# Two chained transformer blocks in float32r halves on one core: TensorE's operands placed at multiples of 64 bytes, the first weight panel on SyncE's queue, weight splits taken out of two waits of the mix stage

## The reference

```python
y = rmsnorm(h, norm_g[layer, 0])
y = gmlp_mixer(y, ...)        # layer 0
y = diff_attention(y, ...)    # layer 1
h = h + rmsnorm(y, norm_g[layer, 1])
y = conv_ffn(rmsnorm(h, norm_g[layer, 2]), ...)
h = h + rmsnorm(y, norm_g[layer, 3])
...
x = x + 0.5 * swiglu(rms_norm(x, ffn1_norm), ...)
u = rms_norm(x, mix_norm) @ w_in
x = x + concatenate([mla_attention(...), moba_attention(...)]) @ w_out
x = x + 0.5 * swiglu(rms_norm(x, ffn2_norm), ...)
return rms_norm(x, final_norm)
```

## Time and profile before

| | before |
|---|---|
| median of 3 runs | 1079.1 us (1078.93 to 1079.15) |
| the profiled execution | 1078.4 us, its span 1076.5 us |
| TensorE matmuls | busy 1064.8 us (99%), 5976 of them |
| TensorE weight loads | busy 910.5 us (85%) |
| VectorE | busy 773.5 us (72%) |
| ScalarE | busy 653.1 us (61%) |
| GpSimd | busy 35.5 us (3%) |
| DMA | 198.13 MB, mean 184 GB/s |
| granted TensorE clock | 0.997 on average |

### The profile page before, as it was taken

How to read it: one execution, slowest core, us unless ns; L and a number is a source line. 1 busy time by engine, 2 the same in 40 slices (tenths; PEclk the granted TensorE clock), 3 DMA queues, 4 the chain that set the end, 5 groups by cost and what they waited for, 6 DMA issues and landing times.

```text
span 1076.5 us, 15631 instructions
## 1 busy us (share of the span) xinstructions
PE 1064.8 (99%) x5976; PEld 910.5 (85%) x5976; DVE 773.5 (72%) x1213; ACT 653.1 (61%) x1176; POOL 35.5 (3%) x39
## 2 busy tenths in 40 slices
PE   8999999999999999999999999999999999999997
PEld 7988888888799878888888888888899878888886
DVE  5888977878767889777788655665676857565554
ACT  5767766557757777566667545545566647454453
POOL 0830000000000000000000000000000000000000
PEclk9999999999999999999999999999999999999999
DMA  9763866566463347555554755556355516565651
GB/s 349 257 209 128 249 201 199 187 189 202 164 223 112 111 161 243 187 200 187 182 190 146 234 198 186 176 192 219 122 174 156 196 59 206 186 183 192 194 174 40
DMA packets 56777, 198.13 MB, mean 184 GB/s; under 512 B 6576, under 2 KB 8536, under 8 KB 56704
## 3 DMA queue, kind: packets, MB, share of 16 engines
q1 hardware_dynamic: 56016, 195.89, 55.6%
q10 hardware_dynamic: 576, 1.05, 0.3%
q0 software_dynamic: 112, 0.20, 0.1%
HBM read 195.35 MB, written 1.25 MB: 183 GB/s over the span
## 4 chain that ended last, share of the span: by engine, by line
PE 95%; ACT 2%; DVE 2%; DMA 1%; issue 0%; ACTq 0%
PE G L1407 28%; PE Y L1487 27%; PE G L1411 14%; PE G L1392 3%; PE G L1393 3%; PE G L1394 3%; PE G L1442 2%; PE G L1443 2%; PE G L1448 2%; PE Y L1482 2%; PE Y L1393 1%; PE Y L1392 1%; PE Y L1394 1%; PE G L1461 1%; PE G L1615 1%; PE Y L1495 1%
## 5 line engine op out<-in xcount | busy, mean ns | idle before, releaser
L868 DVE TENSOR_TENSOR w_low<-raw,w_high 128x1024 fp32r<-128x1024 f32 x352 | 425.0, 1225 | 37.6 <-ACT w_high L448 36.0
L448 ACT CAST w_high<-raw 128x1024 fp32r<-128x1024 f32 x352 | 363.5, 1045 | 12.0 <-DMA raw<-in_panels 8.4
L1407 PE MATMUL G<-x_parts,w_high 128*128 128x512 f32 x1280 | 325.3, 396 | 0.0
L1407 PEld LDWEIGHTS G<-x_parts,w_high 128*128 128x128 f32 x1280 | 233.4, 188 | 49.6
L537 ACT COPY big<-G 128x512 f32<-128x512 f32 x80 | 46.9, 586 | 246.5 <-PE G L1411 246.5
L1411 PEld LDWEIGHTS G<-x_parts,w_low 128*128 128x128 f32 x1280 | 172.9, 188 | 14.6
L962 DVE TENSOR_TENSOR w<-G,big 128x512 f32<-128x512 f32 x80 | 55.3, 691 | 172.2 <-ACT big L537 172.2
L1411 PE MATMUL G<-x_parts,w_low 128*128 128x256 f32 x1280 | 175.9, 280 | 0.0
L1487 PE MATMUL Y<-w_high,a_high 128*128 128x512 f32 x420 | 133.8, 400 | 0.0
L1487 PE MATMUL Y<-w_high,a_low 128*128 128x512 f32 x420 | 132.2, 396 | 0.0
L1487 PE MATMUL Y<-w_low,a_high 128*128 128x512 f32 x420 | 132.0, 395 | 0.0
(11 more groups left out here) (256 smaller groups left out, 1204.0 us busy)
## 6 DMA issues: line engine op xcount, KB each, us to landing
raw<-in_panels SPq DMA_DIRECT2D x351, 512.0 KB, 4.3
gain_pre<-in_gains SPq DMA_DIRECT2D x7, 512.0 KB, 5.7
gain_post<-in_gains SPq DMA_DIRECT2D x4, 512.0 KB, 6.4
big<-in_xT SPq DMA_DIRECT2D x4, 256.0 KB, 7.0
h<-in_x SPq DMA_DIRECT2D x2, 512.0 KB, 6.8
big<-rel_rows SPq DMA_DIRECT2D x8, 128.0 KB, 4.9
raw<-in_panels ACTq DMA_DIRECT2D x1, 512.0 KB, 5.2
big<-in_w_s SPq DMA_DIRECT2D x1, 512.0 KB, 9.2
```

What stands on the lines that cost most here:

```text
L448: s.copy(WH[:, n % RING, :], raw[:, n % RAWS, :]).then_inc(hi, 1)
L868: v.tensor_tensor(WL[:, n % RING, :], raw[:, n % RAWS, :], WH[:, n % RING, :].bitcast(F32), ALU.subtract).then_inc(lo, 1)
L1407: mm(out, WH[:, n % RING, k * P:(k + 1) * P], X2[:, k, :, :], start=k == 0, stop=False, skip_group_check=True)
```

## The change

Three things change. (1) `h` is made after the operands of TensorE and its rows are longer (1040 floats instead of 1026), and `big2` grows to 2080 floats. As built, `x_parts`, `a_high`, `a_low`, `c4_high`, `c4_low`, both gains, `big1` and `big2` then start at multiples of 64 bytes; `cst` stays 32 past one. (2) Panel 0 is loaded on SyncE's queue, between `x_part(0)` and panel 1. (3) Some casts and splits of weight panels move in the lists of ScalarE and VectorE in the mix stage.

```diff
--- before.py
+++ after.py
@@ -103,17 +103,17 @@
         raw = sb("raw", [P, RAWS, W])
         WH = sb("w_high", [P, RING, W], F32R)
         WL = sb("w_low", [P, RING, W], F32R)
-
-        h = sb("h", [P, TT, D + 2])
         X2 = sb("x_parts", [P, KT, 2, T], F32R)
         AH = sb("a_high", [P, KT, T], F32R)
         AL = sb("a_low", [P, KT, T], F32R)
         c4h = sb("c4_high", [P, T], F32R)
         c4l = sb("c4_low", [P, T], F32R)
+
+        h = sb("h", [P, TT, D + 16])
         gP = sb("gain_post", [P, D])
         gN = sb("gain_pre", [P, D])
         big1 = sb("big1", [P, 2048])
-        big2 = sb("big2", [P, 2052])
+        big2 = sb("big2", [P, 2048 + 32])
         big3 = sb("big3", [P, HEADS * SC])
         w3 = sb("w3", [P, 3, 2 * 2 * SC])
         qk = sb("qk", [P, 2, 2, T])
@@ -162,7 +162,7 @@
         sg = big1[:].rearrange("p (k t) -> p k t", k=KT)
         u8 = big2[:, 0:2048].rearrange("p (k t) -> p k t", k=KT)
         xT = big2[:, 0:2048].rearrange("p (k t) -> p k t", k=KT)
-        sqj = big2[:].rearrange("p (t d) -> p t d", t=TT)
+        sqj = big2[:, 0:TT * (D + 2)].rearrange("p (t d) -> p t d", t=TT)
         lows = big2[:, 0:4 * T].rearrange("p (f m t) -> p f m t", f=2, m=2)
         first2 = big1[:, 0:2 * 512].rearrange("p (t c) -> p t c", t=TT)
         wsT = big3[:, 0:D]
@@ -331,7 +331,7 @@
                 sp.dma_start(xT[:, 2 * q:2 * q + 2, :], io["xT"][:, 2 * q:2 * q + 2, :]).then_inc(xt_in[q], 16)
 
             x_part(0)
-            load(1)
+            load(0), load(1)
             x_part(1)
             load(2), load(3)
             x_part(2), x_part(3)
@@ -632,7 +632,6 @@
                 s.activation(qk[:, a % 2, 0, :], bank[:, 0:T], ACT.Copy, scale=DIFF_D ** -0.5)
                 s.copy(qk[:, a % 2, 1, :], bank[:, T:2 * T]).then_inc(qk_r, 1)
 
-            act.dma_start(raw[:, 0, :], io["panels"][0]).then_inc(ld[0], 16)
             act.dma_start(g0[:], io["gain_first"]).then_inc(g0_in, 16)
             act.wait_ge(consts, 1)
 
@@ -814,10 +813,12 @@
             upto(B + 17)
             qk_out(9)
             turned_out(8, 0), turned_out(8, 1)
-            upto(B + 19)
+            upto(B + 18)
             exps(9)
             qk_out(10)
-            turned_out(9, 0), turned_out(9, 1)
+            turned_out(9, 0)
+            upto(B + 19)
+            turned_out(9, 1)
             cast(8)
             upto(B + 21)
             exps(10)
@@ -839,7 +840,8 @@
             upto(B + 31)
             for a in range(12, 16):
                 turned_out(a, 0), turned_out(a, 1)
-                upto(B + 20 + a)
+                if a < 15:
+                    upto(B + 20 + a)
                 if a == 12:
                     exps(13)
                 elif a < 15:
@@ -1366,7 +1368,8 @@
             for a in range(12, 16):
                 if a < 15:
                     combine(a + 1)
-                upto(B + 20 + a)
+                if a < 14:
+                    upto(B + 20 + a)
                 outs(a)
                 if a > 12:
                     low_out(a - 1)
```

## The result

The changed kernel takes **1067.53 us** (median of 4 runs, 1067.17 to 1067.56), the kernel before 1079.01 us in the same session. The ratio is 0.9893 with a 95% interval of 0.9876 to 0.9910: faster by 11.5 us, where 3.3 us were forecast and the range ended at 1074.8 us. The sign was right; the time lies far outside the range.

A forecast was written before the change was run, and what follows sets the result against it. The prediction took TensorE to bound the kernel, with 95% of the chain of waits. Its terms, 2.0 + 0.4 + 0.9 = 3.3 us, taken from 1079.1 us gave 1075.8 us, range 1074.8 to 1077.9 us.

The forecast's parts named there:

- Pace of the matmuls: Weight products, all stages: the new addresses leave 512-column matmuls at 234 ns each; gain taken as 0.
- The first rival: Weight matmuls: both operands aligned stream faster, 213 ns instead of 234, 85 us gone, 991 us in all; chance 7%.
- The third rival: Weight matmuls: operands in phase collide and slow every matmul, 6 us per ns, 1081.8 us at 1 ns; chance 4%.
- The start: First weight matmul and before: g0 no longer queues behind panel 0, so TensorE starts sooner and keeps 2.0 us.
- the matmul of 61.85 us: Sign in the first gated stage: TensorE's matmul after the wait for a_low starts at about 59.9 us.
- Its rival: At the start: g0 gains only its 0.44 us of issue, total 1077.4 us; chance 12%.
- wrong in the mechanism: Sign against the start's explanation: x0_high, ScalarE's first x_parts operation, still waits for the 4 KB load g0.
- the 5.0 to 5.5 named: Sign at the start: ScalarE's first x_parts operation begins at 5.0 to 5.5 us instead of 7.46.
- my bound: Panel 7, late by DMA: its low part lets TensorE come 2.5 us sooner and no more.
- The two pairs: Mix stage: moved casts and splits close TensorE's idle time, 0.4 us at the second attention pair, 0.9 at the last.
- The boundary: After the last pair: late split and loads counted as nothing, with up to 0.3 us of loss kept in the range.
- The three terms: Start 2.0 us, second attention pair 0.4 us and last pair 0.9 us, together 3.3 us.

The follow-up runs named there:

- pace_table: Program without the kernel's computation: rows of float32r matmuls with loaded and streamed operands at varied byte offsets; 226.7 ns at (0, 0), 512 columns.
- all_off32: Changed kernel with 32 bytes put ahead of everything in SBUF, so every TensorE operand lies 32 bytes past a multiple of 64; 1067.43 us.
- lay_only: Kernel before with only the new addresses, panel 0's queue and the casts and splits left as they were; 1070.91 us.
- not_layout: Changed kernel with the old addresses; panel 0 on SyncE's queue and the moved casts and splits stay; 1075.72 us.
- queue_only: Kernel before with only panel 0's load moved to SyncE's queue; 1076.80 us, ratio 0.9980.
- splits_only: Kernel before with only the casts and splits of the two pairs moved; 1077.60 us, ratio 0.9989.

## Why the prediction was wrong

**Pace of the matmuls: this is the step that failed.** It said "Whichever operand is off, the pace is the same, so an offset of the streamed operand alone costs nothing", and took 0 for both operands level. The rows were read rightly: pace_table has 233.2 ns at (0, 32) and at (32, 0). But the two rows are two cases of one thing, the operands 32 bytes apart, and bound nothing for the case in which they are level. Measured, the layout is worth 1075.72 - 1067.43 = 8.3 us (all_off32, of the same session, stands for the changed kernel; 7.7 by lay_only): from not_layout to after, 512 columns gain 5.7 + 5.6 + 2.2 = 13.5 us, and 256 columns lose 2.5 + 2.3 = 4.8.

**The first rival** (both aligned stream faster, 7%) had the right edit and the wrong size: of the 20 ns over 213 it priced, 6.7 go at 512 columns, and at 256 columns 3.3 are added. Its total had a slip besides: 85 us taken from 1079.1 leave 994 us, and 991 is the span less 85. The argument against it ("that a surplus from an odd offset should depend on which one streams") was a guess about the mechanism that no row bore out. **The third rival** (in phase, slower, 4%) was right for the 256-column products: 3.3 ns each. Both happened at once, and the range held neither. The Trainium skill (TensorE: Matmul & The Clock Gate, "Back-to-back issue gap") gives the 216 ns for 512 columns as the gap of a matmul by itself, and about 131 ns for a stream with weight loads. This case agrees with neither: no offset tried here got under 226.6 ns.

**The start: right in size, with one link wrong.** First weight matmul at 7.04 us (forecast near 7), clock at the 2.4 GHz level, the matmul of 61.85 us at 59.90 (59.9). By medians queue_only has the 2.0 us; at the gated stage the profiled executions of queue_only and not_layout are 1.7 and 1.3 us ahead of that of before. Executions with the same start thus differ there by 0.4 us (those of lay_only and splits_only stand 0.6 us behind that of before), so the hit on 59.9 is partly luck. Its rival (0.4 us) is out. "I am wrong in the mechanism if x0_high still waits for g0": it does. g0 no longer lands behind panel 0, which gave the time, but it was still last (4.8 us, the quarter 4.6), and x0_high started at 4.85 us, before the 5.0 to 5.5 named. Panel 7 let TensorE keep 2.8 us, not the 2.5 of my bound, since its cast began at 21.52 instead of 21.91 us.

**The two pairs: right in size.** From before to not_layout TensorE's lead grew by 0.4 us between the gated stage and 842 us and by 0.9 us at the last pair, as the terms had it. The boundary gave nothing back. In the profiled splits_only the terms are 0.4 and 0.9 us; by medians it shows 0.7 us of 1.3, within its interval. The three terms together: not_layout at 1075.72 us, 0.1 under the forecast, which in effect left the layout out. That closeness is partly luck: against its own session's 1078.59 us it gained 2.9 us of the 3.3, and 2.6 by the profiled executions.

## What to carry to other kernels

When an edit moves operands, the price of the new constellation needs a row with that constellation; two rows that agree may be the same case twice, so ask what they have in common. On back-to-back float32r matmuls, measure the pace against the distance of the loaded and the streamed operand modulo 256 bytes with the kernel's own short sequence: long rows at one distance promised 9 us that short runs did not give, block rows promised 12 and gave 8. One layout need not suit all widths: place each kind of panel for the products that load it.

## What the runs showed of the hardware

- Common settled paces are 213.3 + 13.3 = 226.7 or + 20 = 233.3 ns at 512 columns and 106.7 + 6.7, + 10 or + 13.3 (113.3, 116.7, 120.0) at 256, the first figure being the columns at 2.4 GHz; many distances have a mean between them (228.9, 231.4; 117.8, 118.4). At 384 columns 173.3 ns (160 + 13.3) and at 128 columns 111.7 ns, at distance 0 and 32 alike, the two tried.
- At 512 columns the pace depends on the operands' distance, and comes back with 256 bytes (loaded operand moved: 226.7 ns at 0, 256, 512, 768, 1024; 233.3 at 64, 320, 576, 832; but 233.3 at 192 and 228.9 at 448, 704, 960). A common shift of 32 bytes changes nothing (1067.43 against 1067.53 us), one of 16 does (230.0 to 233.3 ns for 226.7).
- At one distance a row can settle in different patterns: 24 products of 256 columns at 64 bytes keep 113.3 or 117.8 ns, depending on whether one or two products of 256 columns stood ahead.
- The 4 KB of g0 took 4.1 us to land with nothing ahead of it in its queue, longer than the 256 KB quarter of xT (3.9 us).
